# Differential attention: the combination of the two softmaxes on GpSimd, and the head squares as one ScalarE instruction per four heads, summed on VectorE

## The reference, cut to what matters

```python
sc = jnp.einsum('bqhcd,bshcd->bhcqs', qb, k).astype(jnp.float32) * scale
p = jax.nn.softmax(sc, axis=-1)
a = (p[:, :, 0] - lam * p[:, :, 1]).astype(v.dtype)
o = jnp.einsum('bhqs,bshe->bqhe', a, v)
...
o = _rmsnorm(o, subln_g) * (1.0 - lam_init)      # over the 128 columns of a head
return o.reshape(b, s, nh * 2 * dh) @ w_out
```

## Time and profile before

| | |
|---|---|
| time, median of 3 runs | 1442.37 us (1442.36 to 1442.38) |
| the profiled execution | 1442.12 us, of which its span 1440.3 us |
| PE busy | 1422.6 us, 99% of the span |
| DVE, ACT, POOL busy | 858.5, 747.9 and 90.9 us |
| share of the chain that ended last | PE 93%, DVE 3%, ACT 1%, POOL 1% |

### The profile page before, as it was taken

The page is one execution under the profiler, slowest core; times in us unless marked ns, Lnnn a source line. Parts: engine busy times, 40 slices in busy tenths (PEclk is TensorE's granted clock), DMA queues, the critical chain, the costliest instruction groups (busy, mean ns, idle before and its releaser), DMA issues.

```text
span 1440.3 us, 20791 instructions
## 1 busy us (share of the span) xinstructions
PE 1422.6 (99%) x6864; PEld 1184.1 (82%) x6864; DVE 858.5 (60%) x1113; ACT 747.9 (52%) x1216; POOL 90.9 (6%) x115
## 2 busy tenths in 40 slices
PE   9999999999999999999999999999999999999999
PEld 7888888778888888888888988888888898888887
DVE  5555575767555565555655665555657756565654
ACT  6444464656444454444546654444545465465553
POOL 2110110012111000000100000000013000000000
PEclk9999999999999999999999999999999999999999
DMA  9877746315655656556463155566565513555551
GB/s 304 245 224 219 219 155 210 118 59 160 190 189 189 203 162 190 189 187 195 157 219 111 37 160 189 188 187 201 181 208 161 176 60 104 178 167 181 184 183 53
DMA packets 189938, 248.21 MB, mean 172 GB/s; under 512 B 15194, under 2 KB 128101, under 8 KB 189760
## 3 DMA queue, kind: packets, MB, share of 16 engines
q1 hardware_dynamic: 187904, 241.35, 53.1%
q0 software_dynamic: 1984, 6.21, 1.9%
HBM read 246.33 MB, written 1.17 MB: 172 GB/s over the span
## 4 chain that ended last, share of the span: by engine, by line
PE 93%; DVE 3%; ACT 1%; issue 1%; POOL 1%; DMA 0%; SPq 0%; ACTq 0%; DVEq 0%; POOLq 0%
PE ps L272 26%; PE ps L274 26%; PE ps L273 26%; PE ps L760 2%; PE ps L796 2%; PE ps L555 1%; PE ps L785 1%; PE ps L285 1%; DVE h L476 1%; PE ps L367 1%; PE ps L962 1%; PE ps L286 1%; PE ps L290 1%; PE ps L332 1%; PE ps L331 1%
## 5 line engine op out<-in xcount | busy, mean ns | idle before, releaser
L265 DVE TENSOR_TENSOR wlo<-raw,whi 128x1024 fp32r<-128x1024 f32 x450 | 549.5, 1230 | 393.4 <-ACT whi L257 393.2
L257 ACT CAST whi<-raw 128x1024 fp32r<-128x1024 f32 x450 | 469.9, 1051 | 361.5 <-PE ps L274 344.9
L272 PE MATMUL ps<-whi,xhi 128*128 128x512 f32 x1280 | 499.9, 391 | 0.0
L274 PE MATMUL ps<-whi,xlo 128*128 128x512 f32 x1280 | 498.2, 389 | 0.0
L273 PE MATMUL ps<-wlo,xhi 128*128 128x512 f32 x1280 | 498.0, 389 | 0.0
L274 PEld LDWEIGHTS ps<-whi,xlo 128*128 128x128 f32 x1280 | 240.2, 188 | 50.3
L272 PEld LDWEIGHTS ps<-whi,xhi 128*128 128x128 f32 x1280 | 240.3, 188 | 49.5
L273 PEld LDWEIGHTS ps<-wlo,xhi 128*128 128x128 f32 x1280 | 240.3, 188 | 49.3
L272 PE MATMUL ps<-whi,thi 128*128 128x512 f32 x400 | 160.5, 401 | 0.0
L274 PE MATMUL ps<-whi,tlo 128*128 128x512 f32 x400 | 156.4, 391 | 0.0
L273 PE MATMUL ps<-wlo,thi 128*128 128x512 f32 x400 | 156.0, 390 | 0.0
(11 more groups left out here) (181 smaller groups left out, 1141.2 us busy)
## 6 DMA issues: line engine op xcount, KB each, us to landing
raw<-in_ffn_wg_dram SPq DMA_DIRECT2D x176, 256.0 KB, 2.9
raw<-in_ffn_wu_dram SPq DMA_DIRECT2D x176, 256.0 KB, 3.1
raw<-in_ffn_wd_dram SPq DMA_DIRECT2D x176, 256.0 KB, 3.0
raw<-in_w_ffn_up_dram SPq DMA_DIRECT2D x88, 256.0 KB, 3.5
raw<-in_w_in_dram SPq DMA_DIRECT2D x80, 256.0 KB, 3.3
raw<-in_diff_w_in_dram SPq DMA_DIRECT2D x48, 256.0 KB, 3.0
raw<-in_na_w_in_dram SPq DMA_DIRECT2D x48, 256.0 KB, 3.1
raw<-in_w_ffn_down_dram SPq DMA_DIRECT2D x44, 256.0 KB, 3.0
```

Of the source, the lines that this page charges most:

```text
L257: nc.scalar.copy(whi[:, s], raw[:, s]).then_inc(s_hi, 1)
L265: nc.vector.tensor_tensor(wlo[:, s], raw[:, s], whi[:, s].bitcast(F32), ALU.subtract).then_inc(s_lo, 1)
L272: nc.tensor.matmul(outs[t], ahi[:, c], whi[:, s, i], start=start, stop=False)
L274: last = nc.tensor.matmul(outs[t], alo[:, c], whi[:, s, i], start=False, stop=stop)
```

## The change

The combination of a task moves from DVE, where it is one instruction, to POOL, where it is two: a multiplication in place of `ex1` by the weight, and an addition into `ex0`. DVE keeps the weight, which now has two buffers, and raises a new semaphore `s_wgt` for POOL. From task 2 on, DVE waits for the combination of the task two before, ahead of the weight's first instruction. The power for a group of heads now stands in POOL's queue behind the combination of task 9, 13 and (for both last groups) 15.

The squares of four heads are one ACT instruction without sums instead of four with sums, and DVE sums them (one TENSOR_REDUCE per group).

```diff
-        wgt = sb("wgt", [P, 2])
+        wgt = sb("wgt", [P, 4])
...
                 if g >= 2:
-                    act.wait_ge(s_sq, g - 1)
-                for hd in range(4):
-                    ins = nc.scalar.activation(sqa[:, (g % 2) * 512 + hd * P:(g % 2) * 512 + (hd + 1) * P],
-                                               ps[:, Y + g, hd * P:(hd + 1) * P], ACT.Square,
-                                               accum_out=sso[:, g // 2, 4 * (g % 2) + hd:4 * (g % 2) + hd + 1])
-                ins.then_inc(s_sq, 1)
+                    act.wait_ge(s_ss, g - 1)
+                nc.scalar.activation(sqa[:, (g % 2) * 512:(g % 2 + 1) * 512], ps[:, Y + g], ACT.Square).then_inc(s_sq, 1)
...
                 dve.wait_ge(s_sq, g + 1)
+                steps.done(nc.vector.tensor_reduce(sso[:, t, c], sqa[:, (g % 2) * 512:(g % 2 + 1) * 512].rearrange(
+                    "p (g c) -> p g c", g=4), AX_X, ALU.add))
                 nc.vector.tensor_tensor(sso[:, t, c], sso[:, t, c], ri[:, t, inv2], ALU.mult).then_inc(s_ss, 1)
...
                     dve.wait_ge(s_ex, 2 * (b + j + 1))
-
-                    steps.done(nc.vector.reciprocal(wgt[:, 0:1], rs[:, t, 2 * p + 1:2 * p + 2]))
-                    steps.done(nc.vector.tensor_scalar(wgt[:, 1:2], rs[:, t, 2 * p:2 * p + 1], wgt[:, 0:1], lam[:, 4:5],
-                                                       ALU.mult, ALU.mult))
-                    nc.vector.scalar_tensor_tensor(out=ex[:, j % NEX, 0], in0=ex[:, j % NEX, 1], scalar=wgt[:, 1:2],
-                                                   in1=ex[:, j % NEX, 0], op0=ALU.mult, op1=ALU.add).then_inc(s_a, 1)
+                    if j >= 2:
+                        dve.wait_ge(s_a, b + j - 1)
+                    steps.done(nc.vector.reciprocal(wgt[:, j % 2:j % 2 + 1], rs[:, t, 2 * p + 1:2 * p + 2]))
+                    nc.vector.tensor_scalar(wgt[:, 2 + j % 2:3 + j % 2], rs[:, t, 2 * p:2 * p + 1], wgt[:, j % 2:j % 2 + 1],
+                                            lam[:, 4:5], ALU.mult, ALU.mult).then_inc(s_wgt, 1)
...
-            for g in range(4):
-                pool.wait_ge(s_ss, g + 1)
-                c = slice(4 * (g % 2), 4 * (g % 2) + 4)
-                rstd(steps, ro[:, g // 2, c], sso[:, g // 2, c], P).then_inc(s_ro, 1)
+            for j in range(NTASK):
+                pool.wait_ge(s_wgt, j + 1)
+                steps.done(nc.gpsimd.tensor_scalar(ex[:, j % NEX, 1], ex[:, j % NEX, 1], wgt[:, 2 + j % 2:3 + j % 2], None, ALU.mult))
+                nc.gpsimd.tensor_tensor(ex[:, j % NEX, 0], ex[:, j % NEX, 0], ex[:, j % NEX, 1], ALU.add).then_inc(s_a, 1)
+                for g in {9: (0,), 13: (1,), 15: (2, 3)}.get(j, ()):
+                    pool.wait_ge(s_ss, g + 1)
+                    c = slice(4 * (g % 2), 4 * (g % 2) + 4)
+                    rstd(steps, ro[:, g // 2, c], sso[:, g // 2, c], P).then_inc(s_ro, 1)
```

More of the change, by code:

```diff
@@ L186, in build @@
         s_a = sem("probs_ready")
+        s_wgt = sem("second_weight_ready")
         s_at = sem("probs_transposed")
```

## The result

The changed kernel took 1453.56 us (median of 4 runs, 1453.39 to 1454.85) against 1442.38 on the same chip, a ratio of 1.0076 [1.0064, 1.0089]. Its profiled execution took 1453.65, with a span of 1451.9, so 11.6 us more of span than before. The forecast was 1450.6: slower, for the reasons given, but 3 us too little.

A forecast was written before the change was run, and what follows sets the result against it. PE was taken to bound the kernel, so only its waits in the differential attention could change; four steps of +1.75, +2.70, +2.5 and +1.25 summed to +8.2 us, 1450.6. The range was 1446.3 to 1454.5.

The forecast's parts named there:

- What bounds the kernel now: Opening claim: PE has 93% of the last-ending chain, and only stretches where PE waits, as in differential attention, can change.
- the circle: Differential attention: a combination depends through PE on the one two tasks before, 3.43 us per two tasks, pacing later tasks.
- POOL prices outside the bounds: Remaining case in the chances: POOL's instructions cost more or less than the bounds given; chance 0.03.
- the dear prices: Upper bounds for POOL's two instructions, 1.55 us together in place of 1.25: +2.4 us over eight combinations.
- small DVE waits: Head norm: small DVE instructions with two SBUF inputs may wait for POOL, 0.75 each, two on the path: up to +1.5.
- To task 2: Step 1, up to task 2's combination: weight at 274.49, done 2.74 later at 277.23, +1.75 us.
- Task 2 to 8: Step 2: circles of 5.38 us for tasks 4 and 6, 4.34 for task 8; 15.10 in all, +2.70.
- Task 8 to 15: Step 3: three circles of 4.34, two powers costing 0.49 each, task 15 1.36 after task 14; 15.36 us, +2.5.
- The end: Step 4, task 15 to PE's going on: +0.49 to POOL's start, +0.76 for group 3's sum; +1.25 us.
- The clock as a rival: TensorE's clock falls, doubling PE's part of a circle seven times: +12 us more, 1462.8; chance 0.04.
- POOL free of the `lo`: Rival: POOL's multiplication isn't held by the `lo` in tasks 2 to 6: +5.1 us, 1447.5; chance 0.20.
- DVE as the bound: Rival: PE has tasks in hand, POOL's longer way is hidden and DVE's relief shows: -2.85 us, 1439.5; chance 0.03.

The follow-up runs named there:

- the last one: The changed kernel with a broadcast TENSOR_TENSOR multiplication on POOL, the old squares, one more task in flight and two `lo` moved: 1444.19 us, ratio 1.0009.

## Why the prediction was right, and where its size was off

*What bounds the kernel now.* That the stage waits and nothing else does, held: all 11.49 us are there. That the circle sets the pace of the later tasks was half right: with one more task in flight the kernel before is no faster, so DVE is full there as well. This didn't touch the sum, since POOL's circle is longer than both.

*The mechanism* (POOL is longer than DVE in a circle that PE, ACT and DVE wait around) is shown: one more task in flight takes back 5.4 us of 11.2 at the same instructions. The circle itself was forecast exactly but for POOL's prices: without a `lo` or a power it measures 4.73, and with the measured prices the forecast's own sum gives 3.43 - 0.79 + 2.09 = 4.73.

*The term that was mis-sized is POOL's multiplication.* It was costed at 0.50 from the rows of one to 32 columns, with bounds of 0.45 to 0.70 given, and measured 0.92, outside the bounds. It makes about 2.9 of the 3.3 us that are missing. The prediction had named a price of its own for such an instruction as a way to fail, and had given POOL prices outside the bounds a chance of 0.03; this is the case that came. That the time lies in the range all the same is in part luck: eight combinations at 0.39 over the forecast are 3.1 us, more than the 2.4 of the dear prices, and they fit only because the range also held 1.5 us for small DVE waits, without which it would have ended at 1453.0. None of those waits came on the path. Between a `lo` and the addition it shows less, since 0.14 of its 0.92 lies under the `lo`. By steps:

- *To task 2.* The weight's second instruction starts at 274.50 (forecast 274.49). The combination is done 3.47 after it, not 2.74: the `lo` is itself held by task 1's addition (+0.47, not foreseen: the earlier trace rows showed a `lo` held in this way, but the sum let only POOL wait), the multiplication ends 0.79 after the `lo`, not 0.50 (+0.29), the addition is 0.03 shorter.
- *Task 2 to 8.* The circles are 5.65, 5.64 and 4.73 where 5.38, 5.38 and 4.34 were forecast: the multiplication twice at 0.29 and once at 0.42, less 0.03 each.
- *Task 8 to 15.* 5.34, 4.74, 5.33 and 1.71, in place of 4.83, 4.34, 4.83 and 1.36. The multiplication and addition give 0.39 three times and 0.35. What is left is 0.61 and 0.59 for the tasks behind a power, where 0.49 each was forecast. That sum was nearly right by two errors: without the sums on DVE it is 0.12 and 0.39, and the sums, costed at nothing under DVE's wait, give 0.48 and 0.20. They delay the maximum of the task that the circle is waiting for.
- *The end.* +1.14 against +1.25, with a clock at 0.50 for 310 to 313 inside. By the starts of the last two powers the two terms are 0.39 and 0.74, where 0.49 and 0.76 were forecast. The clock as a rival (+12) came in small: in this execution it fell only behind PE's longest wait, not in every circle, and in the others at most in two places of this stage.

*The rivals.* POOL free of the `lo` (1447.5) is refuted by multiplications of 1.82 to 1.89. The Trainium skill (SBUF — State Buffer, Who interferes with whom) says that of two instructions which need the same read interface the one that comes second is blocked for the whole of the other; the traces agree in both directions (1.69 in place of 1.22, 1.82 in place of 0.92, 1.09 in place of 0.19), and add that some 0.14 us of the second one's own time lie under the block. DVE as the bound (1439.5), the rival of the other side, didn't occur, as the combination is done 2.10 us after its weight's start even without a `lo`, against the 0.79 that the rival needs. Yet its remark on DVE was the useful one: DVE is the bound of the kernel before, and what pays there is moving DVE's work in time, which gave 1439.92.

## What to carry to other kernels

Before work is moved to a slower engine to relieve a full one, look whether the moved piece stands in a circle that comes back to the same engines within two tasks: its latency then counts in full, and the relief only turns into waits. Take the price of an instruction from a row of the same form and size, since a slope from small rows missed by almost a factor of two, and count what else stands in the new engine's queue. First try to move the full engine's other work, here two `lo` and a norm, into its own idle time.

## What the runs showed of the hardware

- POOL, 128x256 in f32: TENSOR_SCALAR with one operand from memory 0.92 us, with a constant 0.85; TENSOR_TENSOR 0.72 for the addition of two full operands, 0.61 for the multiplication with one of them broadcast. So the form that reads one full operand is dearer than the one that reads two. The Trainium skill (GPSIMD Engine Reference, section 4.1) calls POOL's operations with one input "roughly line-rate", and those with two inputs about half as fast as DVE's. The traces don't agree: the one-input form is the dearer one here. No DVE row has exactly this form and size; the nearest, a TENSOR_SCALAR of 32x256 with a constant, took 0.28 in the kernel before, and DVE's whole combination 0.48.
- `lo` on DVE and POOL's multiplications and additions exclude each other, down to a multiplication of four columns, while DVE's maximum from PSUM runs beside POOL in its usual 0.69. DVE's small two-operand instructions (0.16) took up to 0.33 beside POOL in the changed kernel and up to 0.59 in the last one.
- TensorE's clock fell to its lower level during or behind waits of PE, most of them of 1.87 to 2.72 us, but also behind one of 1.09 (one more task in flight) and one of 0.82 (the old squares), in different places in different executions. In the profiled executions of the kernel before, and of its four variants with one more task in flight or moved `lo`, it didn't fall in this stage. It stayed full behind one of 2.17 us in the changed kernel, at the same place where it fell behind 2.18 in the kernel with spare matmuls. Where the cost could be read it was 0.2, 1.0 and 1.6 us, most where long matmuls followed.
